# YOCO decoder step on one core: weight sums of the output layer stored from another queue, one sum later

## What is computed

```python
def pool_layer(x, ...):
    ...
    y = (mix * jax.nn.silu(z)) @ w_out      # the output layer: (rows, 2048) @ (2048, 1024)
    return x + y, u_ext[:, -POOL_BUF:]

k, v = shared_kv(x, norm_kv_g, w_kv)        # projections of the rows that the output layer wrote
qz = rmsnorm(x, norm_b_g[j]) @ w_in_b[j]
```

## Time and profile before

| | us |
|---|---|
| median of 3 runs | 2963.59 |
| lowest and highest of these | 2957.68 and 2965.09 |
| the profiled execution's own time | 2959.02 |
| its span in the profile | 2957.3 |
| PE busy in the span | 2875.1 |
| granted TensorE clock, mean | 0.993 of full |

### The profile page before, as it was taken

The page is one execution under the profiler, slowest core; times in us unless marked ns, Lnnn a source line. Parts: engine busy times, 40 slices in busy tenths (PEclk is TensorE's granted clock), DMA queues, the critical chain, the costliest instruction groups (busy, mean ns, idle before and its releaser), DMA issues. The chain is left out here.

```text
span 2957.3 us, 45964 instructions
## 1 busy us (share of the span) xinstructions
PE 2875.1 (97%) x17242; PEld 2415.5 (82%) x17242; DVE 1800.2 (61%) x2772; ACT 1401.7 (47%) x2234; POOL 134.3 (5%) x171
## 2 busy tenths in 40 slices
PE   8999999999999999999999999999999999988998
PEld 7888888888987887778888888879999999865787
DVE  3356555564553322476767666588888888654654
ACT  4444344342232222455646454377777777633322
POOL 0000000000000000000000000100000000022311
PEclk9999999999999999999999999999999999999999
DMA  7433433433526777688897878863444444399553
GB/s 254 160 120 121 150 121 121 148 124 108 198 89 218 245 248 244 225 301 283 282 296 252 276 255 255 263 160 86 110 107 103 110 102 120 116 413 407 186 188 107
DMA packets 326493, 567.27 MB, mean 192 GB/s; under 512 B 26761, under 2 KB 205561, under 8 KB 305689
## 3 DMA queue, kind: packets, MB, share of 16 engines
q1 hardware_dynamic: 324257, 564.61, 59.3%
q0 software_dynamic: 2048, 0.14, 0.0%
HBM read 424.69 MB, written 140.70 MB: 191 GB/s over the span
## 5 line engine op out<-in xcount | busy, mean ns | idle before, releaser
L2255 ACT ACTIVATE attn_scores<-attn_scores,attn_lowest 128x1024 f32<-128x1024 f32 (+15 forms) x256 | 306.7, 1202 | 2.7 <-DVE attn_lowest L2313 2.7
L2313 DVE CUSTOM_DVE_ANT_0 attn_scores<-attn_s,region_early 128x1024 f32<-128x1024 f32 (+7 forms) x256 | 216.6, 856 | 69.4 <-PE attn_s L2196 39.0
L273 PE MATMUL pool_acc<-pool_odd_x_hi,pool_wh 128*128 128x512 f32 (+1 forms) x640 | 223.2, 349 | 0.0
L275 PE MATMUL pool_acc<-pool_odd_x_hi,pool_wl 128*128 128x512 f32 (+1 forms) x640 | 222.9, 348 | 0.0
L274 PE MATMUL pool_acc<-pool_odd_x_lo,pool_wh 128*128 128x512 f32 (+1 forms) x640 | 222.9, 348 | 0.0
L273 PE MATMUL outa_acc<-outa_w_hi,outa_g_hi 128*128 128x512 f32 x512 | 202.7, 396 | 15.8 <-DVE outa_g_lo L1202 13.1
L274 PE MATMUL outa_acc<-outa_w_lo,outa_g_hi 128*128 128x512 f32 x512 | 201.0, 393 | 0.0
L275 PE MATMUL outa_acc<-outa_w_hi,outa_g_lo 128*128 128x512 f32 x512 | 200.9, 392 | 0.0
L273 PE MATMUL pool_acc<-even_x,pool_wh 128*128 128x512 f32 x512 | 200.1, 391 | 0.0
L275 PE MATMUL pool_acc<-even_x,pool_wl 128*128 128x512 f32 x512 | 199.3, 389 | 0.0
L274 PE MATMUL pool_acc<-even_x,pool_wh 128*128 128x512 f32 x512 | 199.2, 389 | 0.0
(11 more groups left out here) (371 smaller groups left out, 6961.4 us busy)
## 6 DMA issues: line engine op xcount, KB each, us to landing
region_early<-w_fold SPq DMA_DIRECT2D x110, 1024.0 KB, 6.8
pool_wz<-in_w_in_a SPq DMA_DIRECT2D x18, 2048.0 KB, 8.3
pool_wu<-w_mix SPq DMA_DIRECT2D x16, 2048.0 KB, 7.9
hold_kq<-in_cache_k SPq DMA_DIRECT2D x64, 512.0 KB, 6.9
region_early<-in_cache_v SPq DMA_DIRECT2D x60, 512.0 KB, 6.7
w_fold<-region_early SPq DMA_DIRECT2D x32, 896.0 KB, 5.6
region_early<-gatedT SPq DMA_DIRECT2D x16, 1024.0 KB, 7.8
gatedT<-pool_gates SPq DMA_DIRECT2D x48, 256.0 KB, 2.2
```

The source lines that it names most:

```text
L273: pe.matmul(out, ah, bh, start=first, stop=False)
L275: return pe.matmul(out, al, bh, start=False, stop=last)
L2255: act.activation(part, part, ACT.Exp, scale=-1.0, bias=low[s][:, x:x + 1], accum_out=sums[s][:, i:i + 1]).then_inc(expd, 1)
L2313: dve.tensor_tensor_reduce(sc[s][:, c, a0:a0 + n], s_ps[idx % 2][:, at0:at0 + n], bias[h % 2][:, b0:b0 + n], -SCALE, low[s][:, x - 2:x - 1 ...
```

## The change

The store of an item moves from SP's list to ACT's. ACT stores item x - 1 after it has scaled item x; after the last item it stores that one as well, once DVE is done with it. SP's list for the items is left with the loads alone. The load of the residual rows leaves `step` and becomes `next_x`, which comes behind the items of the block instead of ahead of them. The two buffers `fold` and every size stay as they are.

```diff
-            def store_item(x):
-                kd, k, c = items[x]
-                sp.wait_ge(folded, 4 * x + 4)
-                at = k * HN + c * FN
-                sp.dma_start(D["w_fold"][kd].rearrange("i p n -> p i n")[:, :, at:at + FN], fold[x % 2][:, 0:7, :]
-                             ).then_inc(fold_out[x % 2], 16)
-
             def fold_items(b):
                 for x in items_of(b):
-                    store_item(x)
                     if x + 2 < len(items):
                         load_item(x + 2)
 
-            def step(i, s, ahead, x_ahead):
+            def step(i, s, ahead):
...
-                if x_ahead:
-                    sp.wait_ge(out_sem[s], 16 * i + 16)
-                    load_x(2 * i + s + 2, s)
-
-            step(0, 0, True, True)
+
+            def next_x(b):
+                sp.wait_ge(out_sem[b % 2], 16 * (b // 2) + 16)
+                load_x(b + 2, b % 2)
+
+            step(0, 0, True)
             sp.wait_ge(w_lo, KC)
             sp.wait_ge(sample_mm, KC // LK)
             load_item(0)
             load_item(1)
-            step(0, 1, True, True)
+            next_x(0)
+            step(0, 1, True)
...
             fold_items(1)
+            next_x(1)
             for b in range(2, full - 2):
-                step(b // 2, b % 2, b + 4 < full, True)
+                step(b // 2, b % 2, b + 4 < full)
                 fold_items(b)
+                next_x(b)
...
+            def store_item(x):
+                kd, k, c = items[x]
+                act.wait_ge(folded, 4 * x + 4)
+                at = k * HN + c * FN
+                act.dma_start(D["w_fold"][kd].rearrange("i p n -> p i n")[:, :, at:at + FN], fold[x % 2][:, 0:7, :]
+                              ).then_inc(fold_out[x % 2], 16)
+
             def fold_items(b):
                 for x in items_of(b):
                     kd, k, _ = items[x]
...
                     for r, at in ((k, slice(0, 8, 7)), (k + HK, slice(3, 7, 3))):
                         w = fold[x % 2][:, at, :]
                         act.activation(w, w, ACT.Copy, scale=gain[:, r:r + 1]).then_inc(fold_scaled, 1)
+                    if x:
+                        store_item(x - 1)
+                    if x == len(items) - 1:
+                        store_item(x)
```

More of the change, by code:

```diff
@@ L1123, in on_sp @@
             nxt.load_raw(sp, 1)
-            step(pairs - 1, 0, False, False)
+            step(pairs - 1, 0, False)
             sp.wait_ge(out_sem[0], 16 * pairs)
@@ L1128, in on_sp @@
             nxt.load_raw(sp, 2)
-            step(pairs - 1, 1, False, False)
+            step(pairs - 1, 1, False)
         self.mm, self.added, self.full = mm, added, full
```

## The result

The changed kernel takes 2973.84 us (median of 14 runs), the kernel before 2963.03 (14 runs); the ratio is 1.0036 with an interval of 1.0028 to 1.0045. The forecast was 3000: the sign came out, and so did the mechanism (load and store in turn), but the size was too large by 26 us. The profiled execution took 2973.84 us, its span is 2972.1.

What follows compares the result with a forecast made beforehand. PE bounds the kernel (busy 97%), items pacing its output-layer waits. 941 + 29 x 9.4 + 11 x 3.5 = 1252, plus 30, put the projections at 1282, +39 us, giving 3000 us; range 2970 to 3030.

Steps and rivals of the forecast that it cites:

- The ring: Output layer's two item buffers: load, scaling, store and next load run in turn without overlap; two buffers work as one.
- The period p of 9.4 us: Time per item in the output layer: 3.85 load, 1.1 scaling, 4.45 store; bounds 8.8 and 10.5 us.
- the store's issue behind the scaling: On ACT, the item store was to go out 1.1 us after scaling begins; bounds 0.6 and 1.34.
- The store from issue to next load issue: Item store issued by ACT until SP's next load issue: 4.45 us; bounds 4.3 and 5.3.
- The load: Item load on SP, first issue to start of scaling, with nothing ahead of it: 3.85 us.
- The 4.1 us for the store by the page's fit: Skill page's estimate for an item store, about 2.0 us fixed plus bytes at 436 GB/s; not used.
- The block's own transfers, d of 3.5 us: Residual rows, x1 store and activations, 2.1 MB, delay an item store once a block by 3.5 us; bounds 2 and 5.
- The sum: Output layer: item 2 scaled by 941, last item at 1252, projections at 1282 instead of 1243.4: +39 us.
- the end: Output layer from the end of the last item's scaling to the start of the projections: 30 us.
- SP's issue time, "nothing is won": 32 store issues of 0.47 us move from SP to ACT; SP waited for landings, so no gain.
- The signs of it: Output-layer traces: item loads 9 to 10 us apart, PE waits 35 to 45 us; wrong if stage ends before 1250.
- The faster rival: Output layer: overlap pays, a block takes 20.3 us, below PE's 21.8; 2943 to 2948 us, chance 0.08.

Runs made afterwards that it cites:

- the added wait: Changed kernel plus one wait: ACT stores item x - 1 only when its scaling of item x has ended; 3001.41 us, 1.0131 of the kernel before.

## Why the prediction was right in sign and wrong in size

- *The ring.* Right. The kernel without lag on the same queue and the kernel with lag on the old queue show it from both sides: the lag costs 25 to 27 us on ACT's queue and 38 on SP's.
- *The period p of 9.4 us.* This step failed; p is 7.2 (7.15 in the turn shown). The term that failed first is the store's issue behind the scaling: "The store may go out when the second has begun, 0.6 us in, or after both, 1.3. I take 1.1." It was 0, outside its bounds, as the ACTIVATE and the DMA of 976.68 show, and the added wait confirms it with 30 us of kernel time. The store from issue to next load issue was 3.8 us, not 4.45: rows 7 were measured with a load ahead of it, and its parts, 1.2 + 2.4 + 0.6, give 4.2 and not the 4.3 written. The load was 3.35 us, not 3.85: I called 992.63 to 996.48 a load with nothing ahead, but a store ran behind it. Together 2.25 us an item, 29 times, 65 us too much. The 4.1 us for the store by the page's fit stand there for DMAs that GpSimd issues; this one took 3.8 from ACT.
- *The block's own transfers, d of 3.5 us.* Too small: from 940.92 to 1213.82, the start of the scaling of items 2 and 31, are 272.9 us, less 29 x 7.17 leaves 65 for 11 blocks, 5.9 each. That is 26 us too little. My bound of 5 did not hold it. The store behind a block's transfers lands after 8.3 to 9.3 us instead of 3.8, in ten turns. The load issued just ahead of them shares with them too (4.37 us for the load of 980.53 instead of 3.35), which I had left out. With the added wait, where the store goes out 1.36 us later, d is 5.0: a part of the excess comes from the store going out so early.
- *The sum.* By these two steps the last item should come 65 - 26 = 39 us earlier than forecast, less the 1.2 us by which item 2 was later than forecast. It came 37 us earlier (1215.2 against 1252), which leaves a rest below 1. Behind it the end was 35 us instead of 30: from the last item of block 11 to item 31 passed 16.2 us instead of 22.3, so that product 14 began only 11.2 us ahead of the end of the last scaling (1203.92), not 17.4. So the forecast was held near the result by two errors of opposite sign; with p alone put right it would have been some 2935, too low by 39.
- *SP's issue time, "nothing is won".* Wrong, and a page was quoted for it. With no lag, issuing from ACT makes the kernel 20 us faster than issuing from SP (0.9947 against 1.0013), and 14 us with the rows ahead (0.9953 against 1). What is saved is a place in a list: on SP the store of an item stands behind a load that waits for the store before it, and behind a long issue. No kernel here keeps the stores on SP in another order, so the shares of queue and order are not separated. The Trainium skill ("DMA: Bandwidth & Descriptors", section "Queues, rings and completion order") says each DMA engine goes round between the queues it has work for, packet by packet. The traces agree only in part. Of the store issued at 977.17 on ACT's queue next to nothing had moved by 982 (0.01 MB, while SP's queue moved 1.3 MB from 977.17); only then did both queues move bytes side by side (0.18 and 0.19 MB from 982 to 983).
- *The signs of it.* PE's waits were to grow to 35 to 45 us from block 7; they grew to 17. They start at product 8 (1051.43). The stage ended at 1250.2, at the very bound of 1250 that was to tell right from wrong. The faster rival had the right ceiling, 2943 to 2948, and needed the lag gone to be reached.

## What to carry to other kernels

A store that is delayed by k items takes k buffers away from those that can be filled ahead. With two buffers and a lag of one, as here, the one that is left is loaded and emptied in turn, and a wait of 1.6 us on an idle engine is the cheaper thing. A store that frees a buffer belongs in a list where it doesn't stand behind a wait for another store to land. When a DMA is placed behind compute in an engine's list, and does not need that compute, cost it from the last wait ahead of it, not from the end of that compute. Where a forecast is a sum of terms, check each term against a trace afterwards even if the total is close: here 65 us too much and 26 too little stood in one sum.

## What the runs showed of the hardware

A DMA in ACT's list behind two ACTIVATEs, with its own semaphore met, is issued at the start of the first ACTIVATE (969.53 and 969.53, and so for 30 of the 32 stores of the changed kernel), not 1.34 us later. An issue on SP's queue takes 0.4 to 0.5 us and took 6.12 us with 2.5 MB issued just ahead; on ACT's queue an issue behind the same transfers took 0.37 us (977.17), but its first bytes came some 4 to 5 us later, where the store of 969.53 had them after 1 us. A store of 896 KB in pieces of 1 KB moves at 366 to 395 GB/s when alone and lands after 3.8 us; behind a block's transfers it took 8.3 to 9.3 us in the changed kernel, and up to 11.7 in the kernel with SP's stores without lag and the rows behind.
